# Order of work in the recurrence, head norm and merges of a two-block transformer kernel

## The chip, the cores and the metric

The kernel runs on one core of one Trainium2 chip, as one launch. The metric is the device time of that core in microseconds (us). A core has a matrix engine (TensorE, PE in the profile; its weight loads are the row PEld), VectorE (DVE), ScalarE (ACT), GpSimd (POOL), and SyncE (SP), which here only issues the weight DMAs. Each engine runs its own list of instructions strictly in order, and they meet at semaphores: an instruction that waits holds everything behind it on its engine.

## What is computed

One sequence of 256 tokens and 1024 features in f32 passes through a first block with three branches and a feed-forward part, and then twice through a block with two kinds of windowed attention and a mixture of 16 experts. Cut to what matters here:

```python
h = rmsnorm(x, norm1_g)
x_rnn, g_rnn, dq, dk, dv, fq, fk, fv, f_logit, gates = split(h @ w_in)
y_rnn = gelu(g_rnn) * rg_lru(causal_dwconv(x_rnn))      # recurrence: h[t] = a[t] * h[t-1] + u[t]
y_diff = rmsnorm(diff_attention(dq, dk, dv, lam), diff_subln_g) * 0.8     # the head norm
y_fox = forgetting_attention(fq, fk, fv, cumsum(log_sigmoid(f_logit + fox_b_f)))
g = sigmoid(gates)
m = g[0] * (y_rnn @ w_br_rnn) + g[1] * (y_diff @ w_br_diff) + g[2] * (y_fox @ w_br_fox)   # merge
x = x + m @ w_out
x = x + (gelu(u_gate) * u_val) @ ffn_down               # u = conv(rmsnorm(x) @ ffn_up)
x = rmsnorm(x, final_g)
for l in range(2):
    qa, ka, va, qw, kw, vw, gates = split(rmsnorm(x, norm_mix[l]) @ w_in_2[l])
    merged = g[0] * (dilated(qa, ka, va) @ w_branch_a) + g[1] * (windowed(qw, kw, vw) @ w_branch_b)
    x = x + merged @ w_out_2[l]
    x = x + expert_choice_ffn(rmsnorm(x, norm_ffn[l]))  # 16 experts, 32 tokens each, 12 MB of weights each
out = rmsnorm(x, norm_final)
```

## The kernel before

**Weights.** All weights come as slabs of 128 x 4096 f32 (2 MB), one list in the order of use, issued by SyncE (L2207) into a few slots. Outside the experts a slab is cut into four pieces, and each f32 piece is turned into two fp32r halves: ScalarE copies the high half (`wh`, L1695), VectorE subtracts it and leaves the low half (`wl`, L1071). This pair is called the split of a piece. TensorE then makes each product of three matmuls (L500 to L502): high by high, high by low, low by high. A piece is 24 matmuls of 256 columns, or 12 of 512. The halves lie in few buffers: six in the recurrence, three in the attention and the merges, so that the split of a later piece waits until TensorE has finished an older one (`buffer_plan`). In all three programs `split(t)` stands where TensorE works at piece t, and makes the piece that the buffers allow then, five ahead in the recurrence, two ahead in the merges. A slot of a slab comes free when VectorE has split its last piece.

**First block.** The order is fixed by hand in one program per engine. The recurrence is written as generators: `lru()` on ScalarE and on VectorE is advanced by one step (`next(rnn, None)`) at each piece of the slabs grnn, dq, dk, dv and fv, and GpSimd multiplies the recurrence's input (L2123) and, for the quarters q 1 and 3, its output with the gelu (L2128); VectorE does quarters 0 and 2 (L1222). ScalarE turns each quarter into `YR.h` (L1840) and must wait for its product. The forget gate's two small products (`forget0`, and `forget` at L655) stand among these pieces. Then come eight attention units with 32 filling pieces (fq, fk, gates) between them, by `schedule`: unit i has scores (s), weights (w), transposes (t) and values (v), and the fills use the banks 3 and 7 by `fill_banks`. The order begins f0 f1 s0 f2 f3 f4 s1. Units 4 to 7 carry one step each of `head_norm` on VectorE (squares L1398, sum L1401, reciprocal and product L1407 and L1409), with a square root on ScalarE (L1923) between; after the last unit TensorE transposes the result (L751).

**Merge and projection.** `merge` runs 12 groups in the first block and 8 in a layer, each a product into one PSUM bank, multiplied with its gate and added on VectorE (L1249, L1253, L1255). In the last four groups ScalarE also makes the high half of the merged quarter (`mh`, L1769), and GpSimd (L2146), or VectorE for the last (L1260), the low half. `project` multiplies it with wout (or wo) into the banks 4 to 7.

**Layers.** After six groups of q and k and the four pieces of `va`, TensorE takes the scores of unit 0 (L795) into the banks 0 to 3, and 12 units with 28 fills follow. `rotate` gives the banks of the groups. Expert slabs are used in f32 as they land; three more slots open for them when the attention is done (`att`), three when the merge is (`merge`), two after the projection (`out`).

The waits around the work that is changed are these lines:

```python
                        V.wait_ge(*dve_s["scan", 2 * q + 1])
                        V.wait_ge(*act_s["gr", 3])
...
                A.wait_ge(*(pool_s if q % 2 else dve_s)["y", q])
...
                    A.wait_ge(*dve_s["ms", l, g])
                    e.activation(M.h[:, s, :], raw[:, s, :], ACT.Copy).then_inc(*act_s.mark(("mh", l, n)))
```

## Time and profile before

| | before |
|---|---|
| median of 3 runs | 1900.84 us (1898.82 to 1902.06) |
| profiled execution | 1898.63 us, of which its span is 1896.8 us |
| PE busy | 1563.6 us (82%) |
| DVE busy | 729.3 us (38%) |
| ACT busy | 605.0 us (32%) |
| POOL busy | 85.5 us (5%) |
| mean granted clock of PE | 0.918 |
| read from memory | 566.35 MB, 300 GB/s over the span |

The span runs from the first to the last instruction of one profiled execution. The stages in it, by the lines that run: recurrence with its projections 0 to 137 us, the eight attention units of the first block to 246, merge and projection to 321, feed-forward to 511, layer 0 up to its experts to 770, its experts to 1200, layer 1 to 1457, its experts and the end to 1897. A busy share is an average over all of them; where an engine is idle, the question is what it waited for and whether anything later depends on it. An entry such as "PE bank L500 <- ACT qf L1904: 5.8, 1, 5.8" says that PE, at line 500, waited 5.8 us in all, once, the longest 5.8 us, for what ScalarE did at line 1904.

### The profile page before, as it was taken

What the parts mean: (1) busy time and instruction counts of PE and PEld (TensorE: products, weight loads), DVE (VectorE), ACT (ScalarE), POOL (GpSimd) and SP (SyncE); (2) the same over time, 40 slices, a digit from 0 to 9 for tenths busy, and PEclk for the clock granted to TensorE, in tenths of its full rate; (3) what the DMA queues carried; (4) which work ended last, traced back from release to release, by engine and by line L of the source; (5) the groups of instructions that cost most, each with busy time, mean ns of one, the idle gap of its engine ahead of it and who ended that gap; (6) DMA issues with size and microseconds to landing.
All of it is one profiled execution on the core that took longest, in us unless ns stands there. A gap on an engine that the chain in (4) does not pass through costs nothing.

```text
span 1896.8 us, 32934 instructions
## 1 busy us (share of the span) xinstructions
PE 1563.6 (82%) x14818; PEld 1198.9 (63%) x14818; DVE 729.3 (38%) x1411; ACT 605.0 (32%) x1075; POOL 85.5 (5%) x104
## 2 busy tenths in 40 slices
PE   8989999999999999876666656899998966656655
PEld 7879998999899888542222222788896632222322
DVE  7785667887465656200000000546654100000001
ACT  5755545665454654000000000446642100000001
POOL 2030001000021001000000000001000000000000
PEclk9999999999999999998877787899999988788787
DMA  7433354645454439999999999744369999999997
GB/s 296 158 137 134 134 189 178 222 178 185 164 210 148 145 134 403 410 429 430 430 431 429 431 430 429 294 178 145 128 273 410 429 430 430 430 430 429 431 429 302
DMA packets 45964, 570.58 MB, mean 301 GB/s; under 512 B 6880, under 2 KB 7424, under 8 KB 11392
## 3 DMA queue, kind: packets, MB, share of 16 engines
q1 hardware_dynamic: 39168, 552.62, 71.1%
q0 software_dynamic: 4784, 15.18, 2.3%
q8 instruction: 116, 1.90, 0.4%
q10 hardware_dynamic: 1872, 0.69, 0.1%
q14 instruction: 24, 0.20, 0.0%
HBM read 566.35 MB, written 2.10 MB: 300 GB/s over the span
## 4 chain that ended last, share of the span: by engine, by line
PE 52%; DMA 34%; DVE 7%; ACT 5%; another core or an unknown queue 1%; issue 1%; POOL 0%; SPq 0%; ACTq 0%; DVEq 0%
DMA slab<-in_slabs 34%; PE bank L500 11%; PE bank L501 11%; PE bank L502 11%; PE bank L992 4%; PE bank L1034 2%; DVE wl L1071 2%; ACT wh L1695 2%; PE bank L474 1%; PE bank L971 1%; ACT sx L1983 1%; DVE sx L1295 1%; PE bank L809 1%; PE bank L1047 1%; PE bank L863 1%
## 5 line engine op out<-in xcount | busy, mean ns | idle before, releaser
L992 PE MATMUL bank<-slab,xe 128*32 128x256 f32 x4096 | 312.5, 461 | 155.0 <-DMA slab<-in_slabs 153.6
L1071 DVE TENSOR_TENSOR wl<-slab,wh 128x1024 fp32r<-128x1024 f32 (+1 forms) x286 | 349.3, 1238 | 204.0 <-ACT wh L1695 203.8
L500 PE MATMUL bank<-hth,wh 128*128 128x256 f32 x1344 | 389.2, 290 | 5.8 <-ACT qf L1904 5.8
L501 PE MATMUL bank<-htl,wh 128*128 128x256 f32 x1344 | 381.5, 284 | 0.0
L502 PE MATMUL bank<-hth,wl 128*128 128x256 f32 x1344 | 381.3, 284 | 0.0
L1695 ACT ACTIVATE wh<-slab 128x1024 fp32r<-128x1024 f32 (+1 forms) x286 | 294.6, 1044 | 135.5 <-PE bank L502 135.2
L992 PEld LDWEIGHTS bank<-slab,xe 128*32 128x32 f32 x4096 | 143.4, 127 | 303.5 <-DMA slab<-in_slabs 194.2
L500 PEld LDWEIGHTS bank<-hth,wh 128*128 128x128 f32 x1344 | 258.9, 193 | 20.2 <-issue 19.3
L501 PEld LDWEIGHTS bank<-htl,wh 128*128 128x128 f32 x1344 | 259.1, 193 | 0.1
L502 PEld LDWEIGHTS bank<-hth,wl 128*128 128x128 f32 x1344 | 258.9, 193 | 0.0
L1034 PE MATMUL bank<-slab,ha 128*32 128x256 f32 x2048 | 161.0, 470 | 88.4 <-DMA slab<-in_slabs 82.1
L1034 PEld LDWEIGHTS bank<-slab,ha 128*32 128x32 f32 x2048 | 75.7, 130 | 162.7 <-DMA slab<-in_slabs 107.4
L2083 ACT ACTIVATE ta<-bank 128x256 f32<-128x256 f32 x32 | 12.3, 384 | 500.1 <-PE bank L992 500.1
L1659 DVE COPY ye<-bank 128x256 f32<-128x256 f32 x32 | 13.6, 425 | 269.2 <-PE bank L1034 269.2
L1652 DVE SCALAR_TENSOR_TENSOR ta<-ta,bank 128x256 f32<-128x256 f32 x32 | 13.5, 421 | 260.4 <-ACT ta L2083 260.4
L1655 DVE SCALAR_TENSOR_TENSOR ta<-bank,ta 128x256 f32<-128x256 f32 x32 | 13.6, 424 | 243.7 <-PE bank L992 243.7
L2089 ACT ACTIVATE ha<-bank 128x256 f32<-128x256 f32 x32 | 12.3, 384 | 273.6 <-PE bank L1018 273.6
L1983 ACT ACTIVATE sx<-sx,sm 128x256 f32<-128x256 f32 (+1 forms) x80 | 46.7, 585 | 77.4 <-DVE sm L1524 46.2
L2173 POOL DMA_DIRECT2D bias<-in_bias x56 | 31.7, 571 | 863.8 <-DVE x L1287 443.9
L1047 PE MATMUL bank<-ye,gz 32*128 32x256 f32 x512 | 48.8, 453 | 20.2 <-DVE ye L1659 17.4
L1295 DVE CUSTOM_DVE_ANT_0 sx<-bank,bias 128x256 f32<-128x256 f32 x112 | 40.5, 420 | 39.9 <-PE bank L795 28.9
L1047 PEld LDWEIGHTS bank<-ye,gz 32*128 32x128 f32 x512 | 21.2, 194 | 53.9 <-DVE ye L1659 37.3
(358 smaller groups left out, 2112.2 us busy)
## 6 DMA issues: line engine op xcount, KB each, us to landing
slab<-in_slabs SPq DMA_DIRECT2D x257, 2048.0 KB, 44.3
slab<-in_slabs SPq DMA_DIRECT2D x11, 1024.0 KB, 7.1
bias<-in_bias POOLq DMA_DIRECT2D x56, 192.0 KB, 3.7
x<-in_x SPq DMA_DIRECT2D x2, 512.0 KB, 4.4
rg<-in_rg POOLq DMA_DIRECT2D x1, 1024.0 KB, 9.4
scratch<-rel POOLq DMA_DIRECT2D x4, 256.0 KB, 5.0
out<-x SPq DMA_DIRECT2D x2, 512.0 KB, 2.6
bt<-scratch POOLq DMA_DIRECT2D x1, 768.0 KB, 4.7
```

The source lines that it names most:

```text
L474: e.matmul(bk[b][:, 0:128], ident[:, :], ident[:, :], start=True, stop=True)
L500: e.matmul(o, wh, xh, start=start, stop=False, skip_group_check=True)
L501: e.matmul(o, wh, xl, start=False, stop=False, skip_group_check=True)
L502: return e.matmul(o, wl, xh, start=False, stop=stop, skip_group_check=True)
L992: t = e.matmul(bk[bank][32 * j:32 * j + 32, 0:256], XE[:, c, 32 * ex:32 * ex + 32], w[:, k, 256 * j:256 * j + 256], start=(i == 0 and k == ...
L1034: t = e.matmul(bk[3][32 * j:32 * j + 32, 0:256], HA[q][:, o_:o_ + 32], w[:, k, 256 * j:256 * j + 256], start=(i == 0 and k == 0), stop=(i ...
L1047: t = e.matmul(bk[b][:, (j % 2) * 256:(j % 2) * 256 + 256], GZ[q][rows_, tb * 128:(tb + 1) * 128], YE[q][rows_, :], start=(ex == 0 and m < ...
L1071: e.tensor_tensor(lo, src, hi.bitcast(F32), ALU.subtract).then_inc(*dve_l.mark(p))
L1295: return e.tensor_tensor_reduce(out=S_, in0=ps, in1=bias, scale=0.125, scalar=-3.0e38, op0=ALU.add, op1=ALU.max, accum_out=c_mx[:, st:st + 1])
L1695: e.activation(hi, src, ACT.Copy).then_inc(*act_h.mark(p))
L1983: t = e.activation(S_[:, q * w:(q + 1) * w], S_[:, q * w:(q + 1) * w], ACT.Exp, bias=c_nm[:, st + q:st + q + 1], accum_out=c_dn[:, st + q: ...
L2173: e.dma_start(btiles[n % 6], I["bias"][n]).then_inc(*s_bt[n % 6].mark((l, n), 16))
```

## The change

Nothing is computed otherwise; work is moved in the engines' lists, and to other banks.

- **Forget gate.** TensorE's `forget` (L655) moves from behind the first pair of dq to behind the first pair of dk; VectorE's step after it comes one yield later, and ScalarE's exponential and logarithm move from the first to the second pair of dk.
- **Recurrence.** On ScalarE the recurrence's step now stands behind the split of its piece in dv and fv, not ahead of it. The product of the last quarter (q = 3) moves from GpSimd to VectorE.
- **Fill banks in the first block.** From the first scores on, the pairs of fills with k % 4 = 2 take bank 3 instead of those with k % 4 = 0, so that f2 and f3 go to bank 3, f4 and f5 to bank 7.
- **Head norm.** The sum of squares follows the squares at once (unit 4), the square root moves from unit 6 to unit 5, and the last product from unit 7 to unit 6.
- **Merges.** ScalarE makes the high half of a merged quarter behind the splits of the next group, the last one behind the first split of wout; VectorE's low half of the last quarter moves behind its split of wout's first piece.
- **Banks in the layers.** `va` takes the banks 4 and 5 (before: 0 and 1), and the merge groups 0, 1, 3, 2, 0, 1, 3, 2 (before: 2, 3, 0, 1, 2, 3, 0, 1).

```diff
@@ -410,6 +410,9 @@
     rotate(groups)
+    for l in range(2):
+        rot.update({("va", l, tb): 4 + tb for tb in range(2)})
+        rot.update({("mg", l, n): (0, 1, 3, 2)[n % 4] for n in range(8)})
@@ -430,15 +433,15 @@
-    def fill_banks(sched, late):
+    def fill_banks(sched, late, turn):
...
             if kind == "f":
-                out[k] = out[k - 1] if k % 2 else 3 if seen and k % 4 == 0 else 7
+                out[k] = out[k - 1] if k % 2 else 3 if seen and k % 4 == turn else 7
         return out
-    bank_f, bank_l = fill_banks(sched_f, 0), fill_banks(sched_l, 4)
+    bank_f, bank_l = fill_banks(sched_f, 0, 2), fill_banks(sched_l, 4, 0)
     bank_l[0] = bank_l[3] = 6
@@ -659,7 +662,7 @@
                 reader[rot[key, pr]] = [(act_s, (key, pr))]
-                if (key, pr) == ("dq", 0):
+                if (key, pr) == ("dk", 0):
                     forget()
@@ -1216,7 +1219,7 @@
                                              ALU.add).then_inc(*dve_s.mark(("scan", n)))
-                    if q % 2 == 0:
+                    if q != 1:
                         V.wait_ge(*dve_s["scan", 2 * q + 1])
@@ -1228,7 +1231,6 @@
             gates, raw, tmp = (GT, M1raw, TMP) if l == "f" else (GL, MLraw, TMPL)
-            M = M1 if l == "f" else ML
             if l == "f":
@@ -1237,7 +1239,6 @@
                     V.wait_ge(s, v)
-            last = 3 if l == "f" else 2
             cnt = 0
@@ -1253,17 +1254,17 @@
                 e.tensor_tensor(m, m, x, ALU.add).then_inc(*dve_s.mark(("ms", l, g)))
-                if bi == last - 1:
-                    if n < 3:
-                        continue
-                    V.wait_ge(*act_s["mh", l, n])
-                    e.tensor_tensor(M.l[:, s, :], m, M.hf[:, s, :], ALU.subtract).then_inc(*dve_s.mark(("ml", l, n)))
         def project(l, p, tag):
             J = flat(TMP if l == "f" else TMPL)
+            raw, M = (M1raw, M1) if l == "f" else (MLraw, ML)
             for i in range(2):
                 for j in range(4):
                     split(p + 4 * i + j)
+                    if i == 0 and j == 0:
+                        V.wait_ge(*act_s["mh", l, 3])
+                        e.tensor_tensor(M.l[:, 6:8, :], raw[:, 6:8, :], M.hf[:, 6:8, :],
+                                        ALU.subtract).then_inc(*dve_s.mark(("ml", l, 3)))
                     if i and j == 1:
@@ -1317,6 +1318,7 @@
             yield
+            yield
             V.wait_ge(*pe_s["forget"])
@@ -1396,7 +1398,6 @@
             e.tensor_tensor(SQ, O8, O8, ALU.mult).then_inc(*dve_s.mark("osq"))
-            yield
             V.wait_ge(*dve_s.now)
@@ -1759,14 +1760,24 @@
             raw, M = (M1raw, M1) if l == "f" else (MLraw, ML)
-            last = 3 if l == "f" else 2
-            for g, (bi, n, p, npieces, k_per) in enumerate(merge_groups(l)):
+            groups_ = merge_groups(l)
+
+            def high(g):
+                n = groups_[g][1]
+                s = slice(2 * n, 2 * n + 2)
+                A.wait_ge(*dve_s["ms", l, g])
+                e.activation(M.h[:, s, :], raw[:, s, :], ACT.Copy).then_inc(*act_s.mark(("mh", l, n)))
+            last = len(groups_)
+            for g, (bi, n, p, npieces, k_per) in enumerate(groups_):
                 for j in range(npieces):
                     split(p + j)
-                if bi == last - 1:
-                    s = slice(2 * n, 2 * n + 2)
-                    A.wait_ge(*dve_s["ms", l, g])
-                    e.activation(M.h[:, s, :], raw[:, s, :], ACT.Copy).then_inc(*act_s.mark(("mh", l, n)))
+                if g > last - 4:
+                    high(g - 1)
+            p = first["wout" if l == "f" else f"wo{l}", 0]
+            split(p)
+            high(last - 1)
+            for j in range(1, 8):
+                split(p + j)
@@ -1836,7 +1847,7 @@
                 yield
-                A.wait_ge(*(pool_s if q % 2 else dve_s)["y", q])
+                A.wait_ge(*(pool_s if q == 1 else dve_s)["y", q])
                 e.activation(YR.h[:, s, :], XC[:, s, :], ACT.Copy).then_inc(*act_s.mark(("yr", q)))
@@ -1859,15 +1870,15 @@
                     split(first[key, 0] + 2 * pr + j)
-                if (key, pr) == ("dk", 0):
+                if (key, pr) == ("dk", 1):
                     forget()
...
             for j in range(4):
+                split(first[key, 0] + j)
                 next(rnn, None)
-                split(first[key, 0] + j)
             tokens(key, None, dst, (rot[key, 0], rot[key, 1]), first[key, 0] + 3)
@@ -1918,7 +1929,7 @@
                 first_out(i)
-                if i == 6:
+                if i == 5:
                     A.wait_ge(*dve_s["oms"])
@@ -1927,8 +1938,6 @@
         merge("f")
-        for j in range(8):
-            split(first["wout", 0] + j)
@@ -2055,8 +2064,6 @@
             merge(l)
-            for j in range(8):
-                split(first[f"wo{l}", 0] + j)
             for c in (0, 2):
@@ -2121,7 +2128,7 @@
             e.tensor_tensor(TI[:, s, :], TI[:, s, :], TR[:, s, :], ALU.mult).then_inc(*pool_s.mark(("u", q)))
-        for q in (1, 3):
+        for q in (1,):
             s = slice(2 * q, 2 * q + 2)
```

## Rows read from the trace of the kernel before

**Rows 1.** The page, part 2: tenths in 40 slices of the span.
```profile
PEclk9999999999999999998877787899999988788787
DMA  7433354645454439999999999744369999999997
```
**Rows 2.** Waits from 60 to 100 us: total us, times, longest us.
```profile
PE bank L655 <- DVE fz L1318: 2.9, 1, 2.9
```
**Rows 3.** Windows of 2 us: busy us of each engine, granted clock, DMA share, GB/s.
```profile
84.00:86.00 2.00, 2.00 (x9) 1.82 (x9) 2.00 (x3) 0.00 (x0) 0.00 (x0) 0.50 0.00 0
86.00:88.00 2.00, 2.00 (x16) 2.00 (x15) 1.65 (x4) 0.00 (x0) 0.00 (x0) 0.77 0.64 123
...
136.00:138.00 2.00, 0.92 (x4) 0.95 (x5) 2.00 (x4) 1.98 (x3) 0.00 (x0) 0.50 0.96 385
138.00:140.00 2.00, 2.00 (x12) 2.00 (x11) 2.00 (x9) 0.24 (x1) 0.00 (x0) 0.50 0.95 303
140.00:142.00 2.00, 2.00 (x13) 2.00 (x13) 0.46 (x3) 1.48 (x7) 0.00 (x0) 0.62 0.76 311
```
**Rows 4.** Waits from 100 to 150 us.
```profile
PE bank L500 <- ACT qf L1904: 5.8, 1, 5.8
```
**Rows 5.** Chain of waits, 60 to 150 us: start us, us, what.
```profile
87.20 0.12 PE bank L501
...
128.26 2.78 POOL xc L2128
...
133.59 0.97 ACT vf L1757 x2
...
136.45 0.49 ACT qf L1904
```
**Rows 6.** VectorE in order of time: start, us, what, idle before.
```profile
89.70 1.23 DVE L1071 TENSOR_TENSOR wl<-slab,wh 128x1024 fp32r<-128x1024 f32 x1 [2.01 <-ACT wh L1695]
...
112.93 1.23 DVE L1071 TENSOR_TENSOR wl<-slab,wh 128x1024 fp32r<-128x1024 f32 x1 [3.21 <-ACT wh L1695]
114.07 3.41 DVE L1217 TENSOR_TENSOR_SCAN xc<-aa,ti 128x256 f32<-128x256 f32 x2
...
124.57 0.69 DVE L1222 TENSOR_TENSOR xc<-gr,xc 128x512 f32<-128x512 f32 x1
...
125.78 1.22 DVE L1071 TENSOR_TENSOR wl<-slab,wh 128x1024 fp32r<-128x1024 f32 x1
```
**Rows 7.** TensorE in order of time: unit 0's scores.
```profile
130.38 0.93 PE L673 MATMUL bank<-kd,qd 64*128 64x128 f32 x8
```
**Rows 8.** GpSimd in order of time, 105 to 135 us.
```profile
110.47 6.47 POOL L2123 TENSOR_TENSOR ti<-ti,tr 128x512 f32<-128x512 f32 x4 [68.86 <-ACT tr L1834]
```
**Rows 9.** Waits from 243 to 250 us.
```profile
PE bank L751 <- DVE o L1409: 2.3, 1, 2.3
```
**Rows 10.** VectorE in order of time, 205 to 262 us.
```profile
222.32 2.35 DVE L1071 TENSOR_TENSOR wl<-slab,wh 128x1024 fp32r<-128x1024 f32 x2
224.98 0.56 DVE L1394 COPY pt<-bank 128x384 f32<-128x384 f32 x1 [0.31 <-PE bank L701]
...
229.53 1.22 DVE L1401 TENSOR_REDUCE sm<-sq 128x8 f32<-128x1024 f32 x1
```
**Rows 11.** Waits from 293 to 306 us.
```profile
PEld bank L500 <- DVE wl L1071: 4.1, 3, 1.8
...
PE bank L500 <- DVE wl L1071: 3.0, 3, 1.4
```
**Rows 12.** ScalarE in order of time, 285 to 305 us.
```profile
292.38 0.63 ACT L1769 ACTIVATE m1h<-m1raw 128x512 fp32r<-128x512 f32 x1 [2.87 <-DVE m1raw L1255]
```
**Rows 13.** Waits from 564 to 570 us, layer 0.
```profile
PE bank L795 <- ACT va L1757: 1.3, 1, 1.3
```
**Rows 14.** Waits from 697 to 703 us, layer 0.
```profile
PE bank L500 <- DVE obl L1554: 1.0, 1, 1.0
```
**Rows 15.** SyncE's own waits, 690 to 780 us.
```profile
SPq L2207 <- DVE wl L1071: 57.6, 6, 15.0
```

## The prediction

> **What bounds the kernel now.** I read the page first, its 40 slices. The transfers run at nine tenths or more in the slices 15 to 24 and 30 to 38, counted from 0 [rows 1]: these are the two expert stages, and there every microsecond is a transfer's. Nothing of the change lies in them, so what it is worth is read in the rest, from the start to the experts of layer 0 and in layer 1's mixer. There TensorE is the bound: it is at work nearly throughout, at full clock, and what can be won are the stretches in which it stands. So the second view was the list of waits, one short window after another, for TensorE alone, and the third the windows of 2 us around each, for the clock. The reader is to see six places. At 80 us TensorE waits 2.9 us for VectorE's copy of the forget gate's sum [rows 2]. At 131 us it waits 5.8 us for a bank that ScalarE has not read out [rows 4]. At 246 us it waits 2.3 us for the head norm's last product [rows 9]. From 295 to 305 us it waits three times for a low half, 3.0 us in all [rows 11]. In layer 0 it waits 1.3 us for the copies of va [rows 13] and 1.0 us for the last attention output [rows 14]; layer 1 has the same two waits with the same figures. Behind the first two of these the granted clock is at 1.2 GHz for a while: half of 2.4 GHz from 84 to 86 us and again from 137 to 140 [rows 3]. The expert stages pass on what the mixers win: SyncE's transfers before them wait for VectorE's splits [rows 15], and these for TensorE's pieces through the few buffers, so that the start of the flood of expert slabs moves with TensorE.
>
> **Forget gate, 80 to 88 us.** TensorE's small product moves four pieces later in its list (dq's second pair, dk's first), 11.5 us by 24 matmuls to a piece and 0.12 us to a matmul [rows 5]; what it waits for is made at 83. Its 2.9 us wait goes. With it goes the slow stretch: 2 us at 0.50 and 2 us at 0.77 [rows 3] are 1.0 and 0.5 us of lost work. What is late next there is the split of dq's pieces, made more than 10 us ahead, so nothing. VectorE's step and ScalarE's exponential and logarithm, with two table loads, move down their lists as well; behind them on ScalarE wait the copy of dk's second pair and the splits of fv, and neither is wanted within 7 us. The idle time understates what a stall costs, since the first product after it must load its weights uncovered and the last one's tail is counted as busy: the weight-load row of the same three waits reads 4.1 where the matmul row reads 3.0 [rows 11], 0.35 more for each. Sum 2.9 + 1.5 + 0.3 = 4.7 us.
>
> **Recurrence and f2's bank, 104 to 142 us.** The chain reads backwards: f2 needs bank 7, which f0 and f1 have filled; ScalarE empties it at 136.45 [rows 5], because its list holds before that the copies of fv, four splits and the last quarter of y, and this stands still until GpSimd's product, 2.78 us from 128.26 [rows 5]. The change cuts it at two places. f2 now goes to bank 3, whose last reader is ScalarE's second copy of fv, at 133.59 to 134.56 before [rows 5]; that alone would give 2 us. And ScalarE comes to it sooner: splits no longer wait behind the recurrence's steps (VectorE stood 3.2 us for one at 112.93, and 2.0 us at 89.70 for one that the stall at 80 had held up [rows 6]), and the last product takes 0.69 us on VectorE, as that of q = 2 does [rows 6], for 2.78 on GpSimd, whose queue behind it (four small transfers of the forget rows) also starts sooner. I went through the lists of ScalarE and VectorE once with these edits and the durations of the trace. VectorE ends the splits of f0 and f1 about 6 us sooner, TensorE wants them 4.7 us sooner. Before, the split of f1 was there at 127.0 [rows 6] and wanted at 130.38 - 24 x 0.12 = 127.5 [rows 5, 7]; after, it is some 2 us ahead. The copies of fv end about 125.4, and unit 0's scores about 126.7 (130.38 - 4.7 + 0.93 [rows 7]): f2 starts at once. So the wait goes, 5.8 us plus 0.3, and with it the slow stretch, in which 0.9 us at 0.50, 2 us at 0.50 and 2 us at 0.62 [rows 3] lose 0.5, 1.0 and 0.8 us. Sum 8.4 us; at the least, with the bank's change alone, 2.5 plus nothing of the clock.
>
> **A page on this place.** GpSimd's four products of the recurrence take 6.47 us [rows 8]; the pair of scans that lies in them takes 3.41 us, while the split just before took 1.23, no longer than elsewhere [rows 6]. After the change more of VectorE's list falls into these 6.5 us: the split of fv's third piece and the forget gate's six small steps, some 3.5 us. The Trainium skill (GPSIMD Engine Reference, 8. Key points) says that GpSimd shares its SBUF interfaces with VectorE and contends with those of its instructions that have two SBUF inputs. By that rule splits and steps there would lengthen as the scans do, nearly threefold, and the trace bears it out for scans only. That is the first rival's mechanism; the row of the split is why I do not take it.
>
> **Attention and head norm.** From f2 on TensorE is without a wait up to 245 us, with VectorE and ScalarE paced by it, so the 13 us pass through. The exchange of banks 3 and 7 among the fills only changes the phase. The sum of squares, 1.22 us [rows 10], and a scaling now come at unit 4, ahead of two splits; the first of them ended at about 223.5 (222.32 and half of 2.35) and TensorE came to it at 224.95, when its transposes were done (VectorE's copy starts then [rows 10]). Its cover is thus 1.4 us for a cost of 1.4: between nothing and 0.3 us, I take 0.1. The root and its two table loads move on ScalarE by one unit, in front of a split that has over 2 us to spare. The last product comes at unit 6 and is ready four us before TensorE asks. The wait of 2.3 us [rows 9] goes: 2.3 + 0.2 - 0.1 = 2.4 us. Next on the path is TensorE's own list.
>
> **Merge and projection, 286 to 306 us.** Three buffers: the split of a piece can start when TensorE has ended the piece three before it, 2.9 us of cover. ScalarE, though, first waits for VectorE's sum to make the high half, 2.87 us idle [rows 12], and splits after it; VectorE then has its split behind. With the high half one group later both engines split first: by the same durations the low halves of wout's first pieces come about 3 us ahead of TensorE. VectorE's low half of the last quarter, behind one split, is ready 4 us before TensorE's fourth piece. GpSimd's three subtractions move by a split's 1 us; nobody waits within that. Gain between 3.0 and 4.1 us [rows 11]; I take 3.8, nearer the upper end, for the 0.3 us that each of the three restarts hides.
>
> **Layers.** With va in the banks 4 and 5, unit 0's scores wait for no copy; the first transposes that need these banks come over 15 us later. 1.3 us [rows 13] plus 0.2: 1.5. The first merge group in bank 0 leaves the wait for the last output, which the fourth group takes over, 4 us later, when it is done: 1.0 us [rows 14] plus 0.2: 1.2. The high halves behind splits bring nothing here, as TensorE shows no wait in these merges. Two layers: 5.4 us. The flood starts by as much sooner, and so does the first expert, whose release of a slot the transfers wait for; their distance stays.
>
> **The sum.** 4.7 + 8.4 + 2.4 + 3.8 + 5.4 = 24.7 us; some 0.7 us off for small waits that come up when the large ones go (an estimate, half of the smallest terms' doubt). The profiled execution took 1898.63 us, 1.8 more than its span, and would take 1874.6; it lay 2.2 us below the median of 1900.84, so the forecast is **1877 us**.
>
> **The rivals.** *VectorE becomes the bound in the recurrence.* If its list runs 2 us or more late between 105 and 125 us, by the contention above, TensorE waits at f0 to f3. The scans' stretching applied to 3.5 us of other work adds up to 6 us, less the 2 of cover: 4 us lost, with perhaps 1.5 of clock. Time 1879 to 1883. *The layers' gain is swallowed.* If the flood is held by something else than TensorE's pieces (the slots at the end of attention, or a slab's landing), 3 to 5.4 us are lost: 1880 to 1882. Against it stand SyncE's waits [rows 15]. *f2 still waits.* If ScalarE comes to the copies of fv as late as before but for GpSimd's product, 3 to 8 us stay with their clock: 1880 to 1886. *Slower than before: the clock.* TensorE would run without a pause from 10 to 750 us; were the clock taken down for load, and not only after a pause, each us at 1.2 GHz loses half a us. It decides from 49 us at half clock on (24.6 us lost), and at 60 us gives 1906. Against it: the clock reads nine tenths or more in the first 18 slices, up to 853 us [rows 1], and TensorE works for 600 us of them with no pause but the small waits above.
>
> **How the numbers follow.** The sum as worked out, with the terms' bounds, 1873.5 to 1879.5: 0.58. VectorE bound 0.14, layers swallowed 0.08, f2 waits 0.10. More gained than summed, below 1873.5: 0.06. A clock or other loss that takes nearly all, within 0.2%: 0.02. Slower 0.02. The range of 8 in 10, from 1872.5 to 1884. A measurement of this kernel tells a change from none at about 0.2%, 3.8 us, and all but the last two cases are faster by more: 0.96, 0.02, 0.02.
>
> **What would show it.** Right: no wait of TensorE at L655; f2 straight behind unit 0's scores and the clock full from 13 us to 750; L751 without a wait; wout's pieces evenly apart; L795 and the first merge group without a wait; DMA's full slices starting 24 us sooner. Wrong: a wait of TensorE for wl between 115 and 130 us (first rival), a start of the full transfers that has moved by less than TensorE's last attention unit (second), a wait for ScalarE at f2 (third), clock below full without an idle TensorE ahead (fourth).

## The result, and the profile after

The kernel after takes 1876.87 us (median of 4 runs, 1873.46 to 1879.14) beside 1900.38 us for the kernel before (4 runs): a ratio of 0.9875, 95% interval 0.9856 to 0.9893, 23.5 us. The profiled execution took 1875.89 us with a span of 1874.1.

Each row of before that the forecast wanted gone has this answer. Waits of TensorE at 60 to 290 us, where [rows 2, 4, 9] stood (total us, times, longest us): none. From 293 to 310 us, where [rows 11] stood, and from 560 to 580 us, where [rows 13] stood, its lists are:

```profile
PE bank L477 <- ACT tmp L1713: 1.0, 1, 1.0
```
```profile
PE bank L503 <- DVE wl L1074: 0.7, 1, 0.7
PE bank L822 <- DVE ptl L1546: 0.5, 1, 0.5
```

The first is the norm behind the projection, whose wait of 1.0 us the kernel before had too. The two in layer 0 also stood there before, with the same figures. From 675 to 700 us [rows 14] has no successor.

The windows that answer to [rows 3] (busy us of PE, PEld, DVE, ACT, POOL, then granted clock, DMA share, GB/s):

```profile
84.00:86.00 2.00, 2.00 (x19) 2.00 (x19) 2.00 (x2) 0.89 (x1) 0.00 (x0) 1.00 0.03 8
86.00:88.00 2.00, 2.00 (x19) 2.00 (x18) 1.97 (x5) 1.35 (x2) 0.00 (x0) 1.00 0.63 123
...
136.00:138.00 2.00, 2.00 (x18) 1.67 (x18) 1.03 (x7) 0.32 (x1) 0.00 (x0) 1.00 0.00 0
138.00:140.00 2.00, 2.00 (x19) 2.00 (x18) 0.34 (x3) 1.59 (x7) 0.00 (x0) 1.00 0.00 0
```

TensorE works through at 2.4 GHz in all four, and the mean granted clock from 13 to 748 us reads 1.00. Unit 0's scores start at 126.31 us, for 130.38 [rows 7], f2's first product comes straight behind them, and the clock is full there too:

```profile
126.31 0.93 PE L676 MATMUL bank<-kd,qd 64*128 64x128 f32 x8
127.17 0.38 PE L503 MATMUL bank<-hth,wh 128*128 128x256 f32 x1
```
```profile
126.00:128.00 2.00, 2.00 (x19) 1.53 (x18) 2.00 (x3) 2.00 (x3) 0.00 (x0) 1.00 0.03 8
```

On the page, the granted clock and the transfers show that the stages are the same, each begun sooner; to be held against [rows 1]:

```profile
PEclk9999999999999999998788878999999988877877
DMA  7434456444545259999999999645279999999997
```

SyncE's waits from 670 to 760 us, the same stretch as [rows 15] some 20 us sooner:

```profile
SPq L2214 <- DVE wl L1074: 57.6, 6, 15.0
```

The figure is the same to the tenth: the start of the expert transfers has moved with the splits.

How far TensorE is ahead of before, by the end of the same piece of weights in both traces:

| TensorE at the end of | before, us | after, us | ahead by | step |
|---|---|---|---|---|
| xrnn's third piece | 24.58 | 24.97 | -0.39 | the first transfers' landing |
| dq's third piece (the old stall) | 88.51 | 83.73 | 4.78 | +5.17 |
| dk's third piece (the product's new place) | 100.03 | 95.97 | 4.06 | -0.72 |
| f2 | 142.15 | 130.31 | 11.84 | +7.78 |
| the fill behind the sum of squares | 227.81 | 216.34 | 11.46 | -0.38 |
| first piece of the merge | 251.88 | 238.04 | 13.84 | +2.38 |
| wout's third piece | 307.21 | 289.43 | 17.78 | +3.94 |
| layer 0, first fill behind va | 572.28 | 553.17 | 19.10 | +1.32 |
| layer 0, first merge group | 702.92 | 682.76 | 20.16 | +1.06 |
| layer 1, first piece (behind layer 0's experts) | 1211.81 | 1190.86 | 20.95 | +0.79 |
| layer 1, first fill behind va | 1260.28 | 1238.01 | 22.27 | +1.32 |
| layer 1, first merge group | 1390.92 | 1367.59 | 23.32 | +1.05 |
| end of the span | 1896.8 | 1874.1 | 22.7 | -0.6 |

### The profile page after: what moved, and what is told of

The parts are those of the page before. It is cut to its first block, busy times and chain, and to the rows that moved or that the text cites. A ratio compares the mean times of both kernels' runs of the same rounds, so it can differ in the third digit from the quotient of the medians.

```text
span 1874.1 us, 32930 instructions
## 1 busy us (share of the span) xinstructions
PE 1560.3 (83%) x14818; PEld 1195.6 (64%) x14818; DVE 728.5 (39%) x1412; ACT 606.6 (32%) x1075; POOL 86.0 (5%) x103
## 4 chain that ended last, share of the span: by engine, by line
PE 58%; DMA 34%; DVE 4%; ACT 2%; another core or an unknown queue 2%; issue 1%; SPq 0%; ACTq 0%; DVEq 0%
DMA slab<-in_slabs 33%; PE bank L503 13%; PE bank L504 13%; PE bank L505 13%; PE bank L995 5%; PE bank L1037 3%; PE bank L477 1%; PE bank L974 1%; ACT sx L1992 1%; DVE sx L1296 1%; PE bank L812 1%; PE bank L866 1%; DVE wl L1074 1%; PE bank L835 1%; PE bank L1050 1%
```

## The experiments

A single execution carries the landing of the first transfers with it: xrnn's third piece ended between 24.58 us (before) and 26.15 us in the 14 profiled executions, though no kernel changes anything there. So I compare traces by steps from that piece on, as in the table. Each kernel has one trace. Where two kernels have the same list, most of their steps agree to 0.03 us; there are exceptions of 0.2 to 0.9 us at the forget gate and at f2, and larger ones at the head norm and over the experts, and they are given where they occur.

**The two halves of the change.** The first run keeps what acts up to 142 us, the second the rest.

```diff
 rec_only: before, with these and their counterparts on the other engines
+                if (key, pr) == ("dk", 0):
                     forget()
+                    if q != 1:
+    bank_f, bank_l = fill_banks(sched_f, 0, 2), fill_banks(sched_l, 4, 0)
 rest_only: before, with head norm, merge(l), project and these
+        rot.update({("va", l, tb): 4 + tb for tb in range(2)})
+        rot.update({("mg", l, n): (0, 1, 3, 2)[n % 4] for n in range(8)})
```

> The kernel before with the change's edits up to 142 us alone: forget gate later, the recurrence's steps behind the splits, its last product on VectorE, and the exchange of banks among the fills of the first attention. Head norm, merges and the layers' banks as before. Theory (the gains add): 4.7 and 8.4 us were forecast; the trace after shows 4.45 and 7.8 between the same pieces, so the time falls by about 12 us, to 1888; f2 follows unit 0's scores without a wait, and the waits of 2.3 us at the head norm, of 3.0 us in three at the merge and of 1.3 and 1.0 us in each layer stand as before. Rival (the stages are coupled): with TensorE 12 us sooner, slabs or buffers come too late further on, and the later waits grow; then the fall is under 10 us, and the rest of the change alone would have to win more than 13.

> The kernel before with the other half of the change alone: head norm, high halves of the merges behind the splits, banks of va and of the merge groups. Theory (the gains add): head norm 2.4 less 0.4, merge 3.9, layers 2 x 2.4, together 10.5 us, to 1890; the forget gate's wait of 2.9 us and f2's of 5.8 us stand with their slow stretches. With the other half this gives the whole, 22.7 us of span. Rival (coupled): less than 9 us, or the two halves together off the whole by over 2 us.

Measured: 1887.77 us (4 runs) and 1888.28 us (4 runs) beside 1899.29 us (19 runs), ratios 0.9940 (0.9925 to 0.9954) and 0.9942 (0.9927 to 0.9957). That is 11.5 and 11.0 us, together 22.5 of the 23.5. The steps in the first trace are 4.93, -0.71 and 7.70 us, those of the second 2.38 at the head norm, 3.94 up to wout's third piece, 1.32 and 1.07 in layer 0: as in the kernel after within 0.25. The second also loses 0.33 us at f2, where nothing of its list was changed and the wait is as long as before; its granted clock stays at half for longer there. In the second both waits of the first half stand at their old length:

```profile
PE bank L503 <- ACT qf L1914: 5.8, 1, 5.8
PE bank L658 <- DVE fz L1319: 2.9, 1, 2.9
```

Within the intervals the halves add; the rival of coupled stages falls.

**The forget gate alone.**

```diff
-                if (key, pr) == ("dq", 0):
+                if (key, pr) == ("dk", 0):
                     forget()
```

> The kernel before with only the forget gate's steps moved four pieces later. Theory (TensorE's lead at one wait is lost at the next if the next is set by another engine): the 2.9 us wait and its slow stretch go, 4.5 us are won at 90 us; but f2 waits for ScalarE's copy of the queries, behind y's last quarter, whose chain starts from VectorE's list and not from TensorE, so f2's wait grows from 5.8 us by 2 to 4 and 0.5 to 2.5 of the 4.5 us are left: 1898.5. Rival (VectorE's and ScalarE's lists are paced by TensorE's pieces through the three buffers, and move with it): f2's wait stays at 5.8, and all 4.5 are kept: 1896.

Measured: 1896.16 us (10 runs) beside 1899.38 (13 runs), ratio 0.9984 (0.9975 to 0.9993). The stall and its slow windows are gone, 5.17 less 0.72 us. My theory falls: f2's wait hardly grows, so the other engines' lists do come sooner with TensorE's pieces:

```profile
PE bank L500 <- ACT qf L1905: 6.0, 1, 6.0
PE bank L500 <- DVE wl L1071: 0.2, 1, 0.2
```

At f2 3.4 of the 4.5 us are left: the 0.4 that the waits above are longer, and the rest with the clock, which is at half for longer behind the wait. Another 1.5 go at the head norm, of which more below.

**The clock behind a stall.** Throwaway products fill the two stalls of the kernel before.

```diff
+            for _ in range(n):                      # 13 ahead of forget, 26 ahead of f2
+                e.matmul(bk[b][:, 0:128], ident[:, :], ident[:, :], start=True, stop=True)
```

> The kernel before with throwaway products of a 128x128 identity on TensorE ahead of its two long waits, 13 ahead of the forget gate's second product and 26 ahead of f2; nothing reads what they write, and no wait of the kernel is changed. They should fill 2.8 of the 2.9 and 5.5 of the 5.8 us. Theory (the slow clock follows the idle stretch): the granted clock stays full from 84 to 88 and from 136 to 142 us, and the time falls by what the rows at half clock lost, 1.5 and 2.3 us, 3.8 in all, to 1896.6, though TensorE gets to no product of the kernel sooner by itself. Rival (the clock is taken down for the load on the chip in this stretch, transfers among it, whether TensorE idles or not): the slow windows stay and the time doesn't fall, or rises by what the filling is too long, 0 to 1 us.

Measured: 1896.29 us (10 runs) beside 1899.29, ratio 0.9986 (0.9977 to 0.9996). The same windows as in [rows 3]:

```profile
84.00:86.00 2.00, 2.00 (x15) 1.62 (x14) 2.00 (x2) 0.00 (x0) 0.00 (x0) 1.00 0.03 8
86.00:88.00 2.00, 2.00 (x19) 2.00 (x18) 1.97 (x4) 0.38 (x1) 0.00 (x0) 1.00 0.65 123
...
136.00:138.00 2.00, 2.00 (x19) 2.00 (x19) 2.00 (x8) 0.14 (x1) 0.00 (x0) 1.00 1.03 377
138.00:140.00 2.00, 2.00 (x19) 2.00 (x19) 0.36 (x3) 1.57 (x7) 0.00 (x0) 1.00 0.57 225
```

The transfers run as before, 377 GB/s from 136 to 138 us, and the clock is full: it fell for the idle stretch, not for the load. The steps are 1.55 us at the forget gate and 1.97 at f2, 3.5 for the 3.8 that I had from the half-clock windows.

**The bank alone, and the change without it.**

```diff
-    bank_f, bank_l = fill_banks(sched_f, 0), ...        (bank_only: before, with turn 2)
+    bank_f, bank_l = fill_banks(sched_f, 0, 2), ...     (no_bank: after, with turn 0)
```

> The kernel before with nothing but the exchange of banks 3 and 7 among the fills of the first attention. My step: f2 then waits for ScalarE's second copy of fv, which ended at 134.56, and not for the copy of the queries at 136.5, so 2 to 2.5 us of the 5.8 are won and the clock's slow stretch behind stays for the most part: 1898. Rival: the bank was the whole cause (f2 starts with the scores' end, some 8 us won, 1892). Second rival: nothing is won, since the same reader is only reached by another way (1900).

> The kernel after with the banks of the first attention's fills as before, so that f2 waits again for ScalarE's copy of the queries out of bank 7 and not for the second copy of fv. Theory (the lists' order frees ScalarE, the bank takes the rest of the wait): the copy of the queries comes behind the copies of fv (to 126.5) and the splits of two pieces, at about 128.5 to 129, where TensorE stands ready at 127.4; f2 waits 1.2 to 2 us, and 0.3 for the restart, at full or nearly full clock: 1.5 to 2.5 us slower than after, 1878.9. Rival (with ScalarE free the bank no longer matters): no wait, same time as after within 0.5. Second rival (the bank was the main cause): over 4 us slower, a slow stretch again.

Measured: 1896.06 us for the bank alone (10 runs) beside 1899.29, ratio 0.9980 (0.9971 to 0.9990). Without the bank 1877.87 us (4 runs) beside 1900.78 (7 runs), ratio 0.9875 (0.9857 to 0.9893), which the times can't tell from the kernel after. The waits, of the first and of the second:

```profile
PE bank L500 <- ACT vf L1757: 2.3, 1, 2.3
```
```profile
PE bank L503 <- ACT qf L1915: 1.8, 1, 1.8
```

The bank alone takes the wait from 5.8 to 2.3 us and part of the slow stretch, a step of 3.97 us at f2 where I had 2.5. That the median shows 3.2 is a matter of other places: the forget gate's wait is 3.4 us there for 2.9 [rows 2], at the cost of 0.86, and 1.4 go at the head norm (below). Without it f2 waits 1.8 us, as worked out, and against what I wrote the clock falls behind that:

```profile
130.00:132.00 2.00, 2.00 (x12) 2.00 (x12) 2.00 (x4) 0.89 (x1) 0.00 (x0) 0.56 0.89 328
132.00:134.00 2.00, 2.00 (x13) 2.00 (x12) 2.00 (x7) 0.00 (x0) 0.00 (x0) 0.59 1.04 442
```

That is 2 x 0.44 + 2 x 0.41 = 1.7 us more, and the step at f2 is 3.3 us smaller than in the kernel after. So in the traces the bank is worth 4.0 us alone and 3.3 as the last edit. The spans of the traced executions are 3.8 us apart (1877.9 and 1874.1), the medians 1.0; why the medians differ by less isn't shown, as the other executions have no trace.

**The order of ScalarE's list, and the last product.**

```diff
                 split(first[key, 0] + j)                # no_order: the step ahead of the split again
                 next(rnn, None)
-                    if q != 1:                          # no_y3: the product of q = 3 on GpSimd again
+                    if q % 2 == 0:
```

> The kernel after with ScalarE's steps of the recurrence ahead of its splits again in the pieces of dv and fv, nothing else. Theory (a split stands behind a step that waits for VectorE, GpSimd or a chain of both): the splits of the last pieces of fv and of f0 and f1 come 2 to 4 us later, where TensorE has 1.5 us in hand at f1; it waits 1 to 2.5 us at f1 or f2: 1878 to 1879.5. Rival (this edit has nothing to do with the gain once the last product is on VectorE): same time as after within 0.5.

> The kernel after with the recurrence's last product on GpSimd again (2.78 us for 0.69). Theory: y and with it ScalarE's high half and all behind it, the copies of fv among them, come about 2 us later, to 128.5, and f2, which starts at 127.4, waits about 1 us: 1878. Rival (the product lies beside other work since ScalarE now splits first): same within 0.5. Second rival (the product was the main cause): a wait over 3 us.

Measured: 1879.40 us (4 runs), ratio 0.9884 (0.9868 to 0.9900), and 1878.45 us (4 runs), ratio 0.9880 (0.9866 to 0.9895); the intervals overlap with that of the kernel after, so the verdict is the traces'. Their waits from 60 to 150 us:

```profile
PE bank L503 <- ACT vf L1758: 1.5, 1, 1.5
PE bank L503 <- DVE wl L1074: 0.2, 1, 0.2
```
```profile
PE bank L503 <- ACT vf L1758: 0.4, 1, 0.4
```

By the pieces' ends the order is worth 2.0 us and the product 0.4, where I had 1 to 2.5 and about 1. The product took GpSimd 1.65 us in no_y3, not the 2.78 that I had from [rows 5]; the next part shows what made it longer there. Each of the three edits (bank, order, product) is wanted for a start of f2 without a wait, and taking any one away brings back a part only.

**GpSimd beside VectorE.** In the kernel after, the forget gate's small steps on VectorE fall beside GpSimd's four products (5.91 us from 105.01). First the kernel before, in order of time, then after:

```profile
104.16 0.27 DVE L1327 TENSOR_SCALAR z<-z 8x256 f32<-8x256 f32 x1
104.47 0.41 DVE L1329 TENSOR_TENSOR z<-z,z 8x256 f32<-8x256 f32 x1
...
105.19 0.68 DVE L1332 TENSOR_TENSOR_SCAN z<-z,z 8x256 f32<-8x256 f32 x1
```
```profile
105.30 1.39 DVE L1329 TENSOR_SCALAR z<-z 8x256 f32<-8x256 f32 x1
106.72 1.41 DVE L1331 TENSOR_TENSOR z<-z,z 8x256 f32<-8x256 f32 x1
...
108.44 1.39 DVE L1334 TENSOR_TENSOR_SCAN z<-z,z 8x256 f32<-8x256 f32 x1
109.86 1.20 DVE L1336 TENSOR_SCALAR z<-z 8x256 f32<-8x256 f32 x1
...
111.19 1.25 DVE L1220 TENSOR_TENSOR_SCAN xc<-aa,ti 128x256 f32<-128x256 f32 x2
```

```diff
-            e.tensor_tensor(TI[:, s, :], TI[:, s, :], TR[:, s, :], ALU.mult)      (GpSimd)
+                    e.tensor_tensor(TI[:, s, :], TI[:, s, :], TR[:, s, :], ALU.mult)      (VectorE, ahead of the scans)
```

> The kernel after with GpSimd's four products ahead of the scans (5.9 us from 105.0) made on VectorE instead, about 0.7 us each there, so that GpSimd does nothing beside VectorE's forget steps. In the kernel after, five small steps on 8 partitions take 1.39, 1.41, 1.39, 1.20 us beside GpSimd's products, where they took 0.27, 0.41, 0.68 and 0.28 before with GpSimd idle, and their block 5.9 us for 2.1. Theory (contention between the two engines stretches them): the steps are back at their lengths of before, the block at some 2.2 us; VectorE wins 3.7 us and pays 2.8 for the products, f1's split is ready 0 to 2 us sooner, and the time is the same as after within 0.5, since TensorE has 1.5 us in hand there. Rival (the steps are long because they wait for ScalarE or for one another): they keep 1.2 to 1.4 us and the block its 5.9; f1's split comes 3 us later and TensorE waits about 1.5 us.

Measured: 1877.55 us (4 runs), ratio 0.9876 (0.9862 to 0.9891), as after. The steps are back:

```profile
105.64 0.27 DVE L1331 TENSOR_SCALAR z<-z 8x256 f32<-8x256 f32 x1
105.95 0.42 DVE L1333 TENSOR_TENSOR z<-z,z 8x256 f32<-8x256 f32 x1
...
106.68 0.68 DVE L1336 TENSOR_TENSOR_SCAN z<-z,z 8x256 f32<-8x256 f32 x1
```

The contention is shown. The block takes 2.2 us for 6.0, the four products cost VectorE 2.7, and f1's low half ends at 120.74 us for 121.96 in the kernel after. The time doesn't move, since TensorE comes to f1 later than either.

The four stretched steps end 0.15, 0.27, 0.54 and 0.15 us behind the end of one of GpSimd's products. That is their own length without GpSimd (0.27, 0.41, 0.68, 0.28) less 0.12 to 0.14, as if the step ran when the product was through. It goes the other way as well, and large instructions take part. Of the kernel before, GpSimd and then VectorE:

```profile
111.73 1.29 POOL L2123 TENSOR_TENSOR ti<-ti,tr 128x512 f32<-128x512 f32 x1
112.97 2.33 POOL L2123 TENSOR_TENSOR ti<-ti,tr 128x512 f32<-128x512 f32 x1
...
120.61 1.66 POOL L2128 TENSOR_TENSOR xc<-gr,xc 128x512 f32<-128x512 f32 x1 [3.67 <-DVE xc L1217]
```
```profile
121.03 2.32 DVE L1071 TENSOR_TENSOR wl<-slab,wh 128x1024 fp32r<-128x1024 f32 x1
```

The split at 112.93 [rows 6] began 0.04 us ahead of GpSimd's third product. It kept its 1.23 us, and the product took 2.33 for 1.29. The split at 121.03 began behind a product and took 2.32 us. Of the 286 splits in that trace 14 took over 1.4 us, and each of the 14 lies beside an instruction of GpSimd that began ahead of it. It isn't so for every instruction of GpSimd: beside its TENSOR_SCALAR from 522.73 to 525.59 us a split took 2.09 us and ended first. GpSimd's last product, 2.78 us at 128.26, had a split of VectorE begin beside it at 128.68 that kept its 1.22.

**Trying for more.** TensorE still waits 0.70 us in each layer for a low half, because ScalarE splits that piece only behind unit 1's exponentials. Three kernels move it.

```diff
 early_split = after, and:
+                    if i == 1:
+                        split(fills_l(l)[2][0])         # ScalarE, ahead of layer_exp(l, 1)
+                if kind == "w" and i == 0:
+                    split(fills_l(l)[2][0])             # VectorE, ahead of layer_weights(l, 0)
 early_sum   = early_split, and the yield between osq and osum again, one yield fewer behind oms
 high_only   = early_sum without VectorE's part
```

> The kernel after, and in each layer ScalarE splits the last piece of kw and vw ahead of unit 1's exponentials, for which it stands idle 6.2 us waiting for VectorE's maxima, and VectorE ahead of unit 0's weights. Theory (this 0.70 us wait of TensorE for a low half, at 567 us and again in layer 1, is made by the order of ScalarE's list): the waits go, 0.7 us and 0.3 for the restart in each layer, 1 to 2 us in all: 1875.3. Rival (the exponentials or weights that VectorE now makes 1.2 us later are wanted sooner by TensorE than the piece): nothing is won or up to 1 us lost in each layer.

> As the run with the early split of kw and vw, and the head norm's sum of squares comes at unit 5 again, as in the kernel before, with the root at unit 5 and the last product at unit 6 as after. I had priced that move at 0.1 us; between the traces of before and after TensorE loses 0.4 us there, at the first split behind it. Theory (1.2 us of VectorE's work stand ahead of a split that has less in hand): 0.4 us sooner from 216 us on, and the head norm's wait stays away, since root and product have four us in hand. Rival (the root now waits on ScalarE for the sum, and holds the copies behind it): a new wait of TensorE of 0.5 to 1.5 us between 225 and 245 us.

> The kernel after with ScalarE's split of the last piece of kw and vw ahead of unit 1's exponentials, VectorE's low half left behind unit 0's weights, and the head norm's sum of squares at unit 5. With VectorE's half ahead of the weights as well the wait for the low half was gone in each layer, but the 2 MB slab that this half releases was issued at 564.75 us, ahead of GpSimd's last tiles of the attention bias (issued 563.7 to 566.6, landing 9.0 us later at the median for 3.3 in the kernel after), VectorE stood 2.0 us for them in unit 2's maxima, and TensorE 2.9 us behind that. Theory (what counts is that the slab is issued behind the tiles): the low half ends about 566.4, 0.6 us sooner than after and just behind the last tile's issue; the tiles land in under 4 us, the 0.70 us wait is gone in both layers and no other comes, with 0.4 us from the sum of squares: about 2 us faster than after, 1874.8. Rival (any earlier slab slows the tiles): their median is again above 6 us and TensorE waits 2 to 3 us at unit 1's transposes; 1879 or more.

Measured: 1883.72 us (4 runs), ratio 0.9911 (0.9894 to 0.9928); 1880.43 us (4 runs), ratio 0.9898 (0.9880 to 0.9916); 1884.65 us (6 runs), ratio 0.9921 (0.9907 to 0.9934). Their medians lie 3.6 to 7.8 us above that of the kernel after; the interval of early_sum still overlaps with that of the kernel after, and the single runs of one kernel lie up to 7.3 us apart (1879.41 to 1886.71 for the last). The loss is in the traces: against the kernel after, 3.0 us in each layer for early_split, 3.1 and 3.5 for early_sum, 1.8 and 3.8 for high_only. The wait itself goes each time (0.96 us sooner for the idle 0.70, by the end of the piece that waited), and a larger one comes in its place. Of early_split, VectorE and then TensorE from 560 us on:

```profile
573.87 0.42 DVE L1296 CUSTOM_DVE_ANT_0 sx<-bank,bias 128x256 f32<-128x256 f32 x1 [1.53 <-DMA bias<-in_bias]
...
574.79 0.42 DVE L1296 CUSTOM_DVE_ANT_0 sx<-bank,bias 128x256 f32<-128x256 f32 x1 [0.48 <-DMA bias<-in_bias]
```
```profile
PE bank L822 <- DVE ptl L1546: 3.4, 2, 2.9
```

The issues of that stretch (KB each, median us to landing), of after and of early_split:

```profile
bias<-in_bias POOLq DMA_DIRECT2D x6, 192.0 KB, 3.3
```
```profile
bias<-in_bias POOLq DMA_DIRECT2D x6, 192.0 KB, 9.0
```

VectorE's low half releases a slab of 2 MB. In the kernel after it is issued at 567.04 us, behind GpSimd's six tiles of the bias (begun from 562.9 to 565.8). In early_split it is issued at 564.75, between them (563.7 to 566.6). The two tiles ahead of it landed in 2.6 and 2.7 us, the four behind it in 9.0 to 9.2, and the slab itself took 9.7. The theory for high_only failed on its size: I had counted VectorE's two scalings twice (1.15 us is their sum), so the low half stood right behind them at 563.37, the slab left at 564.61, ahead of the last two of the tiles. These took 9.5 and 9.4 us, the one issued 0.5 us ahead of the slab 6.2, and the first three 2.6 to 2.8:

```profile
564.61 0.33 SPq L2217 DMA_DIRECT2D slab<-in_slabs  x1
```

The median of the six is 4.5 us, below the 6 that the rival named, but VectorE waits for the slowest, and TensorE's waits behind it are 3.2 us in layer 0 and 4.1 in layer 1: the rival held in what counts. A slab held back until the tiles are out wasn't tried. The sum of squares at unit 5 gave its 0.38 us without a wait in both kernels that had it. Alone on the kernel after it would give about that, which the times can't show; it wasn't run alone. No kernel here is shown to be faster than the one after.

## Why the prediction was right

The forecast was 1877.0 us, and 1876.87 was measured. The mechanism was right at all five places: each wait is gone, and so is the slow stretch behind the first two. The profiled execution was to take 1874.6 and took 1875.89. By the steps of the sum:

- **Forget gate**, 4.7 forecast, 4.45 measured (5.17 at the old place, less 0.72 at the new one). The product's own time I had left out on both sides; it is in both traces. The clock's part, 1.5, is the filler's 1.55; with the wait of 2.9 this makes the whole 4.45, so that nothing is left for the 0.3 of restart.
- **Recurrence and f2's bank**, 8.4 forecast, 7.8 measured. Wait and slow stretch are gone, unit 0's scores ended at 127.2 for my 126.7, and the second copy of fv was done at 126.45 for my 125.4, so that f2 started with 0.7 us in hand. The clock's part was 2.0 where I had 2.3, and the restart again nothing. What I had too low was the bank alone, 4.0 for 2.5, as I had given the clock nothing there.
- **VectorE's lead at f1**, 2 us forecast. The low half ended at 121.96, and TensorE came to f1 at about 123.5: 1.5 us. The contention took 3.7 us of VectorE on the forget gate's steps, nearly what the first rival claimed, but the first pair of scans, now behind the products, took 1.25 us for the 3.41 of [rows 6] and gave 2.2 back, and the waits for ScalarE further down the list had room for the rest. The rival's mechanism was right and its end was not. It fell short of TensorE by those 1.5 us. My reason against it was wrong: the split at 112.93 was not stretched because it had begun first, and GpSimd's product paid for it. The Trainium skill (GPSIMD Engine Reference, 8. Key points) names instructions with two SBUF inputs and those in a 2-port perf mode. For the first the trace agrees: the scans were stretched, and so was the split at 121.03, 2.32 us for 1.23. The single-input scalings were stretched too, 1.39 us for 0.27; whether they ran in such a mode no view shows.
- **Head norm**, 2.4 forecast, 2.0 measured: the wait gave 2.38 for my 2.5, the moved sum of squares cost 0.38 for my 0.1. The step that failed is its cover: I took the bound near nothing of a range up to 0.3, and the truth lay just above the range.
- **Merge and projection**, 3.8 forecast, 3.94 measured for waits of 3.0 in all. This is the one place where clearly more came back than the idle time and the slow stretch, 0.3 us for each wait. ScalarE's idle time before the high half is 0.33 to 0.39 us, for 2.87 [rows 12]:

```profile
282.73 0.63 ACT L1769 ACTIVATE m1h<-m1raw 128x512 fp32r<-128x512 f32 x1 [0.38 <-DVE m1raw L1256]
```

- **Layers**, 5.4 forecast, 2.38 and 2.37 measured, 4.75 in all: 1.32 for 1.5 at va, 1.06 for 1.2 at the first merge group. I had put 0.2 of restart on each; at va there was 0.02 of it, at the merge group 0.06. From the first merge group to the end of the layer the lead doesn't change, so the high halves bring nothing there, as said.
- **Expert stages**: they pass the lead on, 0.8 more in one and 0.6 less in the other; over layer 0's experts kernels that change nothing there gained 0.5 to 1.3 us on before or lost 0.4, so that this is their scatter. The second rival falls. The 0.7 that I took off for small waits was not such waits but the terms' own excess and the later first transfers.

The rival of a clock taken down for load falls by the windows above and by the filler. Its opposite, that stalls take it down, carries 3.5 of the 23.5 us. Luck had a share. By the steps the change gained 22.9 us where the sum had 24.7, before the 0.7 taken off. The term that was mis-sized is the restart: 1.6 us of it stood in the sum outside the merge, and the traces show 0.2 there. The 0.7, put down to something else, made up for about two fifths of the 1.8. The rest is hidden in the medians, which are 23.5 us apart where the two traced spans are 22.7, with runs of the kernel after from 1873.46 to 1879.14: that the forecast was met to 0.2 us is chance.

## What to carry to other kernels

Price a stall of TensorE as its idle time plus the slow windows behind it, and expect a faster middle to move the other engines with it where they are tied to its pieces by a few buffers. Before a piece is split sooner to save a short wait, look at what its release lets start: a large transfer sent ahead of small ones that are wanted soon costs more than the wait did. Where VectorE and GpSimd both read SBUF at once, as here, count the time of the one that begins later from the end of the other: a small step can cost a whole product, unless another engine has the slack to pay for it.

## What the runs showed of the hardware that I had not expected

- **The same stall costs the clock or not.** The head norm's wait is 2.3 us in the traces of the kernel before and of bank_only, filler and forget_only. In the first the clock stays full behind it; in the other three it falls, and the lead over before shrinks by 1.4 to 1.5 us right there. Of bank_only:

```profile
244.00:246.00 2.00, 0.77 (x4) 0.77 (x5) 1.18 (x1) 0.00 (x0) 0.00 (x0) 0.70 0.00 0
246.00:248.00 2.00, 2.00 (x11) 2.00 (x10) 0.79 (x2) 1.45 (x3) 0.13 (x1) 0.50 0.00 0
```

  In rec_only, with the same wait, it stays full again. In no_bank a wait of 1.8 us brought it down, in no_order one of 1.5 didn't. The new waits of the last three kernels do both: behind the 2.9 us of early_split in layer 0 it falls, behind the 3.2 us of high_only it doesn't. Early_split, then high_only:

```profile
582.00:584.00 2.00, 2.00 (x11) 1.41 (x11) 0.42 (x1) 0.60 (x1) 0.00 (x0) 0.50 0.73 139
```
```profile
580.00:582.00 2.00, 2.00 (x18) 1.59 (x18) 1.23 (x2) 0.67 (x2) 0.00 (x0) 1.00 0.29 57
```

  What decides between them stays open, and with one trace of each kernel also whether it goes with the kernel or with the execution. So a forecast should carry a stall's clock term as a chance. The traces of bank_only, filler and forget_only contain one such loss each; whether their medians (gains of 3.0 to 3.2 us) do isn't shown.
- **VectorE and GpSimd took turns** beside GpSimd's products of two tiles in SBUF. Of two such instructions the one that began later ended behind the other by about its own length: steps of 0.27 to 0.68 us became 1.20 to 1.41, a split 2.32 for 1.23, and GpSimd's product 2.33 for 1.29 where the split had begun first.
- **A 2 MB transfer** issued among six tiles of 192 KB: the two tiles ahead of it landed in 2.6 and 2.7 us, the four behind it in 9.0 to 9.2, where all six took 2.6 to 3.5 with the slab behind them.
